# Second layer, widest window group of the samples: scores formed on VectorE from the loaded key pages instead of on TensorE from transposed pages

## What is computed

```python
D_WINDOWS = ((128, 1), (512, 4), (2048, 16))   # (window, dilation) of groups 0, 1, 2; 8 heads of 64
def dilated_sample(q, k_ext, v_ext, dil, nback):
    idx = Lb + jnp.arange(T)[:, None] - dil * jnp.arange(nback + 1)[None, :]
    kg, vg = k_ext[:, idx], v_ext[:, idx]
    logits = jnp.einsum('bqhe,bqkhe->bhqk', q, kg) * (HD_D ** -0.5)
    lse = jax.nn.logsumexp(logits, axis=-1)
    p = jnp.exp(logits - lse[..., None])
    return jnp.einsum('bhqk,bqkhe->bqhe', p, vg), lse
```

## Time and profile before

| | |
|---|---|
| median of three runs | 1824.38 us (1821.59 to 1824.96) |
| the profiled execution, its own time | 1821.89 us |
| its span, first to last instruction | 1820.3 us |
| mean granted TensorE clock | 0.998 |
| busy: TensorE, VectorE, ScalarE, GpSimd | 97%, 50%, 32%, 9% |
| the twelve side steps i = 0 to 11 (second round of tiles) | about 900 to 1025 us of the span |
| the side steps i = 12 to 23 (third round) | about 1050 to 1181 us |
| one tile with a full side step of group 2 | 10.92 us |

### The profile page before, as it was taken

How to read it: one execution, slowest core, us unless ns; L and a number is a source line. 1 busy time by engine, 2 the same in 40 slices (tenths; PEclk the granted TensorE clock), 3 DMA queues, 4 the chain that set the end, 5 groups by cost and what they waited for, 6 DMA issues and landing times.

```text
span 1820.3 us, 37580 instructions
## 1 busy us (share of the span) xinstructions
PE 1765.6 (97%) x15399; PEld 1643.6 (90%) x15399; DVE 919.0 (50%) x1396; ACT 583.0 (32%) x1137; POOL 161.3 (9%) x224
## 2 busy tenths in 40 slices
PE   7998999999999999999899999999999999999998
PEld 6995766899999999999888888878789999999998
DVE  4336775654353434443544644577674535343354
ACT  4114556432121222321533533363233212122222
POOL 0700000220000000120000000003002000000001
PEclk9999999999999999999999999999999999999999
DMA  8219998246767676452467657723133666432221
GB/s 273 70 64 366 356 357 326 93 146 247 253 235 269 225 261 230 161 210 75 122 208 238 209 189 241 240 74 110 48 123 116 231 251 245 182 96 72 89 85 60
DMA packets 167166, 338.88 MB, mean 186 GB/s; under 512 B 9179, under 2 KB 116501, under 8 KB 165438
## 3 DMA queue, kind: packets, MB, share of 16 engines
q1 hardware_dynamic: 164691, 249.74, 40.5%
q0 software_dynamic: 2240, 87.41, 12.8%
q10 hardware_dynamic: 114, 0.03, 0.0%
HBM read 324.36 MB, written 100.19 MB: 233 GB/s over the span
## 4 chain that ended last, share of the span: by engine, by line
PE 89%; DVE 5%; ACT 3%; issue 1%; SPq 1%; DMA 1%; ACTq 0%; DVEq 0%
PE pp L654 54%; PE pp L964 16%; PE pp L714 3%; PE pp L1074 2%; PE pp L1121 2%; PE pp L1087 1%; PE pp L913 1%; PE pp L748 1%; PE pp L728 1%; ACT e_p L2076 1%; PE pp L990 1%; PE pp L1102 1%; PE pp L1146 1%; DVE rnorm L1259 1%; PE pp L833 1%
## 5 line engine op out<-in xcount | busy, mean ns | idle before, releaser
L1856 ACT ACTIVATE whi<-raw 128x1024 fp32r<-128x1024 f32 x208 | 220.6, 1061 | 841.9 <-PE pp L654 685.1
L654 PE MATMUL pp<-a_hi,whi 128*128 128x288 f32 x1280 | 275.6, 297 | 1.0 <-DVE zbuf L1272 0.7
L654 PE MATMUL pp<-a_hi,wlo 128*128 128x288 f32 x1280 | 274.4, 296 | 0.0
L1229 DVE TENSOR_TENSOR wlo<-raw,whi 128x1024 fp32r<-128x1024 f32 x208 | 256.2, 1232 | 36.0 <-ACT whi L1856 35.9
L654 PE MATMUL pp<-a_lo,whi 128*128 128x288 f32 x1280 | 274.2, 296 | 0.0
L654 PE MATMUL pp<-b_hi,wlo 128*128 128x288 f32 x1152 | 246.7, 296 | 0.0
L654 PE MATMUL pp<-b_hi,whi 128*128 128x288 f32 x1152 | 246.6, 296 | 0.0
L654 PE MATMUL pp<-b_lo,whi 128*128 128x288 f32 x1152 | 246.6, 296 | 0.0
L654 PEld LDWEIGHTS pp<-a_hi,whi 128*128 128x128 f32 x1280 | 206.4, 189 | 2.3 <-issue 1.6
L1288 DVE TENSOR_TENSOR x<-x,pp 128x576 f32 (+1 forms) x80 | 60.3, 754 | 292.9 <-PE pp L654 281.8
L654 PEld LDWEIGHTS pp<-a_hi,wlo 128*128 128x128 f32 x1280 | 206.5, 189 | 0.0
(11 more groups left out here) (283 smaller groups left out, 2116.8 us busy)
## 6 DMA issues: line engine op xcount, KB each, us to landing
kvring<-in_cache_b_kv SPq DMA_DIRECT2D x128, 512.0 KB, 5.5
out_new_d_sample<-in_cache_d_kv POOLq DMA_DIRECT2D x32, 2040.0 KB, 8.4
raw<-in_w_up SPq DMA_DIRECT2D x32, 1024.0 KB, 5.4
raw<-in_w_down SPq DMA_DIRECT2D x32, 1024.0 KB, 4.9
kring<-in_cache_d_kv SPq DMA_DIRECT2D x104, 256.0 KB, 3.0
vring<-in_cache_d_kv SPq DMA_DIRECT2D x104, 256.0 KB, 4.7
raw<-in_w_in_cd SPq DMA_DIRECT2D x24, 1024.0 KB, 5.2
out_new_d_sample<-in_cache_d_kv POOLq DMA_DIRECT2D x8, 2016.0 KB, 8.3
```

Source lines behind the costliest of these rows:

```text
L654: last = pe.matmul(acc_h[s][:, h, :], w[s][:, k, :], m[:, k, NH * h:NH * h + NH], start=(at_ == 0 and n == 0), stop=(at_ == KT_N - 1 and n ...
L1229: dve.tensor_tensor(wlo_v[j], raw_v[q // 2][:, :, j, :], whi_v[j].bitcast(F32), ALU.subtract).then_inc(wlo_ready, 1)
L1856: act.activation(whi_v[j], raw_v[q // 2][:, :, j, :], ACT.Copy).then_inc(whi_ready, 1)
```

## The change

For steps 0 to 15 the key pages are no longer transposed. Once, in side step 0, four transposes and a copy put the group's 64 query rows into `qtok2` (64 rows, 512 columns: 8 heads of 64). For each page, one matmul (`s_query`) with one column of the identity, repeated 128 times, as its fixed operand spreads that page's query row over all 128 partitions of PSUM bank 4 or 5. VectorE then multiplies the page as it was loaded with that bank into `prod2` and sums over each head's 64 products into one column for each head of `st2` (`s_page`). After two steps `st2` holds a sequence's 64 rows of scores, keys along the partitions. One transpose of it (`s_scores2`) gives the scores, 128 keys wide; a maximum, an exponential and one transpose (`s_weights2`) follow once a sequence instead of once a step, and no mask is needed. ScalarE's copy of the transposed weights scatters them into `pt_g2`, in which each page's weights stand alone between zeros, so that the product with the values (`s_values2`, 16 matmuls as before) can add up page by page. This product comes one side step later (i - 4). The two halves of a sequence are added without a rescale. A key buffer is now free when VectorE has summed the page (`s1_kt_d`). Steps 16 to 31 keep their form and change banks only: the scores go to bank 7, the pages to banks 4 and 5, the product to bank 5. GpSimd lays out no queries for group 2 and clears `st2` and `pt_g2` once.

```diff
+            def query_rows():
+                pe.wait_ge(qs_saved, 4)
+                for t in range(4):
+                    last = pe.transpose(bank[4][0:NS, P * t:P * t + P], q_s[:, 2, t, :], ident)
+                last.then_inc(s1_kt_ps, 1)
+            def s_query(i, p):
+                j = PAGE0[i] + p
+                row = 8 * STEPS[i][1] + STEPS[i][2][p]
+                pe.wait_ge(s1_kt_d, max(1, j))
+                pe.matmul(bank[4 + j % 2], ident[0:NS, row:row + 1].broadcast_to([NS, P]), qtok2[0:NS, :], start=True,
+                          stop=True).then_inc(s1_kt_ps, 1)
+            def s_scores2(i):
+                pe.wait_ge(s1_kt_d, KT_D[i + 1])
+                at_least(pe, s1_e, i - 1)
+                pe.transpose(S1_SC[:, 0:P], st2[:, :], ident).then_inc(s1_s, 2)
+            def s_weights2(i):
+                pe.wait_ge(s1_e, i + 1)
+                at_least(pe, s1_pt, i - 1)
+                at_least(pe, s1_o, i - 1)
+                pe.transpose(S1_WT[:, 0:P], e_s1[:, 0:P], ident).then_inc(s1_pt_ps, 2)
...
+            def s_page(i, p):
+                j, q = PAGE0[i] + p, STEPS[i][2][p]
...
+                dve.wait_ge(k1_loaded[j % NK], 16 * (j // NK + 1))
+                dve.wait_ge(s1_kt_ps, 1 + j + 1)
+                link(dve.tensor_tensor(prod2[j % 2][:, :], kring1[j % NK][:, :], bank[4 + j % 2], ALU.mult))
+                dve.tensor_reduce(st2_v[:, :, 0, :, q], prod2[j % 2][:, :].rearrange("p (t h d) -> p t h d", t=4, h=2),
+                                  AX.X, ALU.add).then_inc(s1_kt_d, 1)
...
-                    if k == 0 and 3 <= i < N_ST + 3:
+                    if k == 0 and i == 0:
+                        query_rows()
+                    if k == 0 and 4 <= i < 20:
+                        s_values2(i - 4)
+                    if k == (2 if i == 19 else 0) and 19 <= i < N_ST + 3:
                         s_values(i - 3)
-                    if k == 1 and 2 <= i < N_ST + 2:
-                        s_weights(i - 2)
-                    if k == 2 and 1 <= i < N_ST + 1:
-                        s_scores(i - 1)
+                    if k == (1 if i > 19 else 2) and softmax1(i - 2):
+                        (s_weights2 if i - 2 < 16 else s_weights)(i - 2)
+                    if k == 2 and softmax1(i - 1):
+                        (s_scores2 if i - 1 < 16 else s_scores)(i - 1)
                     if i < N_ST and 3 <= k < 3 + len(STEPS[i][2]):
-                        s_keys(i, k - 3)
+                        (s_query if i < 16 else s_keys)(i, k - 3)
```

More of the change, by code:

```diff
@@ L256, in build @@
         kt1 = at("kt1", W_B + 6144, 2048)[:, :].rearrange("p (i g n) -> p i g n", i=4, g=4)
+        prod2 = [at(f"prod2{u}", W_B + 6144 + 512 * u, 512) for u in range(2)]
+        qtok2 = at("qtok2", W_B + 7168, 512)
+        st2 = at("st2", W_B + 7680, P)
+        st2_v = st2[:, :].rearrange("p (t r h q) -> p t r h q", t=4, r=2, h=2)
         orun1 = at("orun1", W_B + 8192, 1024)
@@ L375, in build @@
         PAGE_STEP = [n for n in range(N_ST) for _ in STEPS[n][2]]
-        KT_A = [sum(max(1, len(st[2]) // 2) for st in STEPS[:n]) for n in range(N_ST + 1)]
-        KT_D = [sum(len(st[2]) // 2 for st in STEPS[:n]) for n in range(N_ST + 1)]
+        KT_A = [sum(max(1, len(st[2]) // 2) for st in STEPS[16:n]) for n in range(N_ST + 1)]
+        KT_D = [1 + sum(len(st[2]) // (1 if st[0] == 2 else 2) for st in STEPS[:n]) for n in range(N_ST + 1)]
+        softmax1 = lambda n: 16 <= n < N_ST or (0 <= n < 16 and n % 2 == 1)
+        units1 = lambda i: [n for n in (i - 4, i - 3) if 0 <= n < N_ST and (n < 16) == (n == i - 4)]
         part1 = lambda n: n % 2 if n < 16 else n // 8
-        staged1 = lambda n: n // 2 if n < 16 else n - 8
-        last_of = lambda e: 2 * e + 1 if e < 8 else e + 8
-        S1_KT, S1_SC, S1_WT, S1_OUT = (bank[4], bank[7]), bank[5], bank[6], bank[7][:, 0:P]
+        staged1 = lambda n: n - 16
+        last_of = lambda e: e + 16
+        S1_KT, S1_SC, S1_WT, S1_OUT = (bank[4], bank[5]), bank[7], bank[6], bank[5][:, 0:P]
+        S1_OUT2 = bank[6][:, P:2 * P]
         T_SIDE = T_CD + 12
@@ L598, in _ @@
                     cd_unit(8 + i // 2)
-                if 3 <= i < N_ST + 3:
-                    for j in range(PAGE0[i - 3] + NV, min(PAGE0[i - 2] + NV, PAGE0[N_ST])):
+                for n in units1(i):
+                    for j in range(PAGE0[n] + NV, min(PAGE0[n + 1] + NV, PAGE0[N_ST])):
                         load_page(sp, 1, j)
@@ L1032, in prompt_attention @@
                 else:
[L1033 removed]
+                    at_least(pe, s1_kt_a, KT_A[end])
                     pe.wait_ge(s1_kt_d, KT_D[end])
[L1035 removed]
+                    pe.wait_ge(s1_e, end - 1 if end > 16 else end - 2)
                     pe.wait_ge(s1_pt, end - 2)
[L1037 removed]
+                    pe.wait_ge(s1_o, end - 3 if end > 16 else end - 4)
                 token_major(1 + gi, pk[:, 12:16, :], vt, g)
@@ L1056, in prompt_attention, with s_values2 @@
                         group_product(p, bank[6 + d % 2])
+            def query_rows():
[18 more added lines that the diff above has]
+                pe.transpose(S1_WT[:, 0:P], e_s1[:, 0:P], ident).then_inc(s1_pt_ps, 2)
+            def s_values2(i):
+                pe.wait_ge(s1_pt, i // 2 * 2 + 2)
+                at_least(pe, s1_o, i)
+                for p in range(4):
+                    j, q = PAGE0[i] + p, STEPS[i][2][p]
+                    pe.wait_ge(v1_loaded[j % NV], 16 * (j // NV + 1))
+                    for t in range(4):
+                        at_ = 136 * t + 16 * q
+                        last = pe.matmul(S1_OUT2[32 * t:32 * t + 32, :], pt_g2[:, at_:at_ + 32],
+                                         vring1[j % NV][:, P * t:P * t + P], start=(p == 0), stop=(p == 3))
+                last.then_inc(s1_o_ps, 1)
             def s_keys(i, p):
@@ L1062, in s_keys @@
                 on_dve = p % 2 == 1
+                if i == 16 and p == 0:
+                    pe.wait_ge(s1_kt_d, KT_D[16])
                 pe.wait_ge(k1_loaded[j % NK], 16 * (j // NK + 1))
@@ L1637, in s_keys, with query_rows @@
             def s_keys(i, p):
-                dve.wait_ge(s1_kt_ps, PAGE0[i] + p + 1)
-                dve.tensor_copy(kt1[:, :, p, :], bank[7].rearrange("p (i n) -> p i n", i=4)).then_inc(s1_kt_d, 1)
+                dve.wait_ge(s1_kt_ps, 1 + PAGE0[i] + p + 1)
+                dve.tensor_copy(kt1[:, :, p, :], bank[5].rearrange("p (i n) -> p i n", i=4)).then_inc(s1_kt_d, 1)
+            def query_rows():
+                dve.wait_ge(s1_kt_ps, 1)
+                dve.tensor_copy(qtok2[0:NS, :], bank[4][0:NS, :]).then_inc(s1_kt_d, 1)
+            def s_page(i, p):
+                j, q = PAGE0[i] + p, STEPS[i][2][p]
+                if j == 0:
+                    dve.wait_ge(q_zero, 3)
+                if q == 0:
+                    at_least(dve, s1_s, i)
+                dve.wait_ge(k1_loaded[j % NK], 16 * (j // NK + 1))
[3 more added lines that the diff above has]
+                                  AX.X, ALU.add).then_inc(s1_kt_d, 1)
             def s_maximum(i):
                 g, b, _ = STEPS[i]
-                j, w = part1(i), 512 if i < 24 else P + 3 * NS
+                j, w = part1(i), P if i < 16 else 512 if i < 24 else P + 3 * NS
                 dve.wait_ge(s1_s, i + 1)
-                if j < 3:
+                if j == 2:
                     sv = S1_SC.rearrange("p (g n) -> p g n", n=P)
[L1649 to L1653, removed]
+                    link(dve.tensor_tensor(sv, sv, cc("rm1").unsqueeze(2).broadcast_to([P, 4, P]), ALU.add))
+                    link(dve.tensor_tensor(sv[:, :, 0], sv[:, :, 0], cc("k01"), ALU.add))
+                elif j == 3:
                     link(dve.tensor_tensor(S1_SC[:, 0:8], S1_SC[:, 0:8], cc("g0m"), ALU.add))
@@ L1668, in s_output @@
                 b = STEPS[i][1]
-                al, su, run = alpha_s[:, i % 4:i % 4 + 1], sum_s[:, i % 4:i % 4 + 1], run_s[:, b:b + 1]
+                u = i if i >= 16 else i // 2 * 2 + 1
+                al, su, run = alpha_s[:, u % 4:u % 4 + 1], sum_s[:, u % 4:u % 4 + 1], run_s[:, b:b + 1]
                 o = orun1[:, P * b:P * b + P]
@@ L1774, in side @@
             def side(i):
-                if 3 <= i < N_ST + 3:
-                    s_output(i - 3)
-                if 1 <= i < N_ST + 1:
+                if i == 0:
+                    query_rows()
+                for n in units1(i):
+                    s_output(n)
+                if softmax1(i - 1):
                     s_maximum(i - 1)
-                for p in (1, 3) if i < 24 else ():
+                for p in range(4) if i < 16 else ():
+                    s_page(i, p)
+                for p in (1, 3) if 16 <= i < 24 else ():
                     s_keys(i, p)
@@ L2128, in s_weights @@
                 act.wait_ge(s1_pt_ps, i + 1)
-                at_least(act, s1_o_ps, i)
+                if i < 16:
+                    if i == 1:
+                        act.wait_ge(q_zero, 3)
```

(13 more changed lines are left out.)

41 lines of the change are left out of this document (25 added, 16 removed).

## The result

| | before | changed |
|---|---|---|
| median | 1824.67 us | 1851.97 us (1848.88 to 1854.40) |
| ratio to before, 95% interval | | 1.0152 (1.0131 to 1.0173) |
| span of the profiled execution | 1820.3 us | 1848.6 us |

The changed kernel is 1.5% slower.

A forecast was written before the change was run, and what follows sets the result against it. TensorE was taken as the bound, busy throughout the stretch: 79.4 + 2.1 + 0.4 - 54.5 = +27.4 us, plus 0.3, gives 1849.6 from the profiled run or 1852.1 from the median; predicted 1851, range 1840 to 1860.

The forecast's parts named there:

- The query at 1.24 us: On TensorE, each of 64 query matmuls standing alone between dense groups costs 1.24 us, 79.4 us in all.
- the lower end of 1.05: Cheapest price taken for a query matmul on TensorE: 0.95 us plus 0.10 for the slower first pair behind it; 67.2 us in all.
- The second rival: On TensorE, switching rows is cheaper with 64 than with 8: 1.05 us a query, about 1839 us; 10 in 100.
- The single transposes at 0.13 us: On TensorE, 16 transposes of `st2` and of the exponentials, one per side step, add 2.1 us.
- The removed work, 54.5 us: TensorE loses group 2's key transposes (28.5 us), scores (19.0) and transposes of the weights (7.0) over 16 steps.
- A full side step at 12.6 us: In the second round, a tile with its full side step takes 12.6 us in place of 10.92.
- VectorE at 1.43 us a page, with cover: VectorE's multiply and sum take 1.43 us a page, about 8.5 us of work a side step; no query waits.
- The cover of 0.58 us: In odd side steps, VectorE's running sum ends 0.58 us before TensorE's transpose of the weights needs it; price nothing.
- The 0.3 us for the late page: Behind the second round's last tile, VectorE's late page delays the prompt's attention once, up to 0.6 us, taken as 0.3.
- third rival: VectorE late at 2.3 us a page: TensorE waits in odd side steps, 3 to 10 us more, 1854 to 1861; 8 in 100.
- The value pages, costed at nothing: Value pages stand in SP's list behind key buffers freed about 1.5 us later; this was costed at nothing.
- The first rival: On TensorE, a query costs 0.445 us like the transposes, time about 1800 us, break-even 0.81 us a query; 3 in 100.

## Why the prediction was right, point by point

- **TensorE is the bound.** Right. TensorE is busy for all of the stretch before and after, and doubling the query adds its whole 0.86 us 64 times over (55 us by starts, 56.6 by the run times).
- **The query at 1.24 us.** Measured 1.25 to 1.26 in the changed kernel. The choice of L1146 over L793 was right, and so was its reason, the switch to fewer rows. The size of the switch was not: the lower end of 1.05 put it at 0.19, and the runs show 0.39 over a passage of 0.86. The 0.95 us between L793 and its successor was read as a price without a switch, but the successor stands on 64 rows, so it holds the switch's first half: 0.95 - 0.86 = 0.09 us, as much as the way into a query takes more on 64 rows (978.92 - 978.56 = 0.36) than on 128 (988.95 - 988.68 = 0.27). The 0.85 us that the prediction estimated and set aside for the rows is the passage, within 0.01; what it leaves out is the switch. The second rival, 1839, mixed the two up: a query without any switch gives 1827.
- **The single transposes at 0.13 us.** Measured 0.12.
- **The removed work, 54.5 us.** Not measured alone. With 64 x 1.25, 16 x 0.12 and the 0.9 of the value pages (below) the sum is +28.8; the span grew by 28.3, the medians by 27.3.
- **A full side step at 12.6 us.** 12.66.
- **VectorE at 1.43 us a page, with cover.** A page takes 1.41 us (0.69 and 0.69, the second starting 0.72 after the first). The price of nothing was right. The cover of 0.58 us was too small by 0.29, mainly since three instructions were laid end to end that in fact overlap, by 0.23 us in all, and the running sum is 0.07 shorter. The 0.3 us for the late page ahead of the prompt's attention did not show: from 900 to 1090 us TensorE's waits are the four of the kernel before (1.6, 1.5, 0.2 and 0.2 us in total).
- **VectorE late (third rival).** Its place was right and its price wrong. At 2.8 us a page it cost 64 us, where the prediction had some 6.4 us for each 0.1 beyond 2.5, about 19, and took no account of the clock.
- **The value pages, costed at nothing.** Wrong by 0.9 us. Among TensorE's waits in the changed kernel from 1080 us on there is one that was not there before:

```profile
PE pp L1178 <- DMA vring<-in_cache_d_kv: 0.9, 1, 0.9
```

  In side step 19 the products of steps 15 and 16 stand two dense groups apart. The last page of step 16 can be loaded only when the product of step 15 has freed its buffer, so it comes late once.
- **The busy times.** VectorE grew by 40.4 us where some 45 were forecast; the mask and the wide maximum that go had been weighed too lightly. The periods behind side step 20 are 10.92 us again, as before.
- **The first rival, a query as cheap as transposes.** It fell as a statement on this matmul: 0.86 us is the least that 512 columns of plain float32 cost in these runs. Among matmuls of one kind, too, the rows show hardly any gain from size: four of 512 columns cost 1.19 us and 16 of 128 columns 1.21. But its break-even of 0.81 us was the right question. On 128 rows the query at 0.86 brings the kernel to within 0.3% of before, and at 0.24 it is faster.

## What to carry to other kernels

Before a transpose is traded for a matmul, price both by starts in the trace: four float32 transposes of 128 columns cost 0.445 us, one float32 matmul of 512 columns 0.86, and 0.39 more when it stands alone on fewer rows than its neighbours. Where a product only picks a row, a high and a low part stacked on the full rows pick it in one matmul of the dense kind, 0.24 us. What an engine off the path may grow by for nothing is the time between its last result and the place where that is waited for, here 0.87 us, and it shrinks as soon as the bound engine gets faster.

## What was not expected of the hardware

A switch between 128 and 64 rows costs TensorE 0.39 us each time, there and back, seen as late weight loads (0.17 us idle ahead of the query and 0.76 behind it, against none ahead and twice 0.24 behind on 128 rows). And in the kernel with the multiply issued three times, waits of TensorE in a list that is otherwise full went with half the granted clock over the queries behind them, 2.07 us in place of 1.12, so that waits of some 20 us in all went with a loss of 71 in the profiled execution. The length of the wait alone does not tell: the clock fell behind waits of at most 0.70 us there, and stayed at 1.00 from 915 to 1030 us in the kernel with split rows and the multiply issued twice, whose waits reach 1.4 us.
